# How the background steps of the first attention layer are dealt over the attention loop

## The reference

```python
def gqa_attend(q, k, v):
    s = jnp.einsum('bqhgd,bkhd->bhgqk', q, k).astype(jnp.float32) * (GQA_HEAD_DIM ** -0.5)
    p = jax.nn.softmax(s, axis=-1).astype(v.dtype)
    return jnp.einsum('bhgqk,bkhd->bqhgd', p, v)
...
    k, v, q, g = jnp.split(h @ p["w_in"], cuts, axis=-1)
    q = apply_axial_rope(rms_norm(q.reshape(B, S, GQA_KV_HEADS, GQA_GROUP, GQA_HEAD_DIM), p["q_norm"]), cos, sin)
...
    o = sweep_query_blocks(lambda qb: gqa_attend(qb, k_all, v_all), q).reshape(B, S, GQA_WIDTH)
    y = (o * jax.nn.silu(g)) @ p["w_out"]
```

## Time and profile before

| what | us |
|---|---|
| median of 3 runs | 4112.04 (4110.61 to 4112.57) |
| the profiled execution | 4113.06, of which the span is 4111.2 |
| TensorE busy, whole span | 3764.8 (92%), mean granted clock 0.965 |
| VectorE, ScalarE, GpSimd busy | 1603.5 (39%), 1214.8 (30%), 527.4 (13%) |
| first attention layer's loop, from the first maximum to the last | 1799.6 to 2859.6 |
| one token tile in it (tiles 3 to 8) | 117.9 to 119.4 |
| the last tile, first to last maximum | 94.5 |

### The profile page before, as it was taken

How to read it: one execution, slowest core, us unless ns; L and a number is a source line. 1 busy time by engine, 2 the same in 40 slices (tenths; PEclk the granted TensorE clock), 3 DMA queues, 4 the chain that set the end, 5 groups by cost and what they waited for, 6 DMA issues and landing times.

```text
span 4111.2 us, 56888 instructions
## 1 busy us (share of the span) xinstructions
PE 3764.8 (92%) x24715; PEld 2348.1 (57%) x24715; DVE 1603.5 (39%) x2422; ACT 1214.8 (30%) x2101; POOL 527.4 (13%) x499
## 2 busy tenths in 40 slices
PE   8899999989799999988989888988898999989989
PEld 4566666565477777344555555555554666556654
DVE  2444454543311111733444444444223444444430
ACT  1323323310111111423233333333122444344430
POOL 0211222111000000411001000100112000200001
PEclk9999999999799999998999999998999999999989
DMA  3000000212599999930000000002100000000002
GB/s 106 17 17 22 17 17 12 83 34 103 232 362 367 368 365 350 366 95 16 11 6 16 16 16 16 11 20 97 68 16 11 1 1 12 1 1 1 1 31 72
DMA packets 108049, 346.80 MB, mean 84 GB/s; under 512 B 13351, under 2 KB 39271, under 8 KB 89623
## 3 DMA queue, kind: packets, MB, share of 16 engines
q1 hardware_dynamic: 85862, 284.85, 19.0%
q0 software_dynamic: 9072, 33.03, 2.4%
q10 hardware_dynamic: 12864, 25.27, 1.7%
HBM read 296.94 MB, written 46.19 MB: 83 GB/s over the span
## 4 chain that ended last, share of the span: by engine, by line
PE 77%; DVE 10%; issue 5%; ACT 3%; POOL 3%; DMA 2%; SPq 1%; POOLq 0%; ACTq 0%; DVEq 0%
PE ps L2522 10%; PE ps L2018 8%; PE ps L1613 7%; PE ps L383 7%; PE ps L3226 6%; PE ps L2540 4%; PE ps L2045 4%; PE ps L1630 4%; PE ps L2914 3%; PE ps L1207 3%; DVE sb L1992 2%; PE ps L457 2%; PE ps L3188 2%; POOL sb L1825 2%; PE ps L468 1%
## 5 line engine op out<-in xcount | busy, mean ns | idle before, releaser
L2522 PE MATMUL ps<-sb 128*128 128x512 f32 x960 | 472.5, 610 | 55.4 <-DVE sb L2682 22.1
L2018 PEld LDWEIGHTS ps<-sb 128*128 128x128 f32 x2624 | 299.9, 144 | 340.4 <-ACT sb L2026 130.5
L2026 ACT ACTIVATE sb<-ps 128x512 f32<-128x512 f32 x400 | 238.9, 597 | 797.6 <-PE ps L2018 797.6
L2018 PE MATMUL ps<-sb 128*128 128x128 f32 x2624 | 429.3, 287 | 47.7 <-ACT sb L2002 18.5
L2002 ACT ACTIVATE sb<-ps,sb 128x1280 f32<-128x1280 f32 (+1 forms) x288 | 352.4, 1230 | 143.8 <-DVE sb L1995 140.9
L383 PE MATMUL ps<-sb 128*128 128x512 f32 x704 | 358.9, 625 | 5.1 <-DMA sb<-in_w_in 3.6
L1613 PE MATMUL ps<-sb 128*128 128x256 f32 x1504 | 343.0, 382 | 0.8 <-ACT sb L1645 0.8
L3226 PE MATMUL ps<-sb 96*128 96x512 f32 (+1 forms) x768 | 339.0, 535 | 0.0
L2033 DVE COPY sb<-ps 128x512 f32<-128x512 f32 x256 | 177.1, 692 | 414.0 <-PE ps L2018 413.7
L2045 PEld LDWEIGHTS ps<-sb 128*64 128x64 f32 x5248 | 290.1, 139 | 72.4 <-ACT sb L2026 37.0
L2045 PE MATMUL ps<-sb 128*64 128x128 f32 x5248 | 325.6, 279 | 2.9 <-DVE sb L2033 1.6
(11 more groups left out here) (361 smaller groups left out, 4671.4 us busy)
## 6 DMA issues: line engine op xcount, KB each, us to landing
sb<-in_exp_gate SPq DMA_DIRECT2D x47, 1024.0 KB
sb<-in_exp_up SPq DMA_DIRECT2D x47, 1024.0 KB
sb<-in_exp_down SPq DMA_DIRECT2D x47, 1024.0 KB
sb<-in_l_w_mod ACTq DMA_DIRECT2D x12, 2048.0 KB
d_ys<-sb SPq DMA_DIRECT2D x47, 512.0 KB, 14.4
sb<-d_x SPq DMA_DIRECT2D x32, 512.0 KB, 4.1
sb<-in_w_in SPq DMA_DIRECT2D x22, 512.0 KB, 4.1
sb<-in_x SPq DMA_DIRECT2D x16, 512.0 KB, 5.0
```

Of the source, the lines that this page charges most:

```text
L2018: ins = k.pe.e.transpose(k.bank(6)[:, 128 * j:128 * j + 128], self.Pb[g % 2][:, 1280 * b + 128 * c:1280 * b + 128 * c + 128], k.f(C_ID, 128))
L2026: k.act.e.activation(self.PT[:, xs[0]:xs[-1] + 1, :], k.bank(6)[:, 0:128 * len(xs)].rearrange("p (j t) -> p j t", j=len(xs)), ACT.Copy).th ...
L2522: ins = pe.e.matmul(k.bank(5), lhs[:, kk, :], w[:, kk, 512 * half:512 * half + 512], start=kk == 0, stop=kk == 7)
```

## The change

The step costs `cost` (us of TensorE) are given for the six kinds that use bank 5. `dealt` goes through the same steps in the same order. Each such step is put at the place where its share of the summed cost falls. If the step in front of it is in that place already, it goes to the next one, except that the steps kk > 0 of a product may stay with their neighbours. All other steps stay at the place of the step in front of them: an evacuation directly behind its last matmul, and likewise loads, squares, roots and `silu`. The order of TensorE's background steps stays the same; the slots' gaps no longer count.

```diff
+    cost = dict(mmq=0.9, mmg=0.9, mmo=0.9, turnh=0.55, qturn=0.5, gT=0.5)
+
+    def dealt(todo, count):
+
+
+        steps = [s for slot in todo for s in slot]
+        kinds = [s[1] if s[0] == "lat" else s[0] for s in steps]
+        total = sum(cost.get(x, 0.0) for x in kinds)
+        out, place, last, done = [[] for _ in range(count)], 0, -1, 0.0
+        for step, kind in zip(steps, kinds):
+            if kind in cost:
+                place = max(place, int(done / total * count))
+                if place == last and not (kind[:2] == "mm" and step[3]):
+                    place = min(place + 1, count - 1)
+                last = place
+                done += cost[kind]
+            out[place].append(step)
+        return out
...
-                    yield from (s for slot in todo[place * len(todo) // max(last, 1):] for s in slot)
-                    todo, place, last = window(n), 0, sum(places(x) for x in range(g, g + 8))
+                    todo, place = dealt(window(n), sum(places(x) for x in range(g, g + 8))), 0
...
-                    for slot in todo[place * len(todo) // last:(place + 1) * len(todo) // last]:
-                        yield from slot
+                    if place < len(todo):
+                        yield from todo[place]
                     place += 1
```

More of the change, by code:

```diff
@@ L2486, in everything @@
             yield from slot
-        todo, place, last = [], 0, 0
+        todo, place = [], 0
         for g in range(-1, G + 1):
```

## The result

The changed kernel takes 4052.36 us (median; 4046.87 to 4056.85 over four runs) against 4111.93 before: a ratio of 0.9857, with a 95% interval of 0.9845 to 0.9870. That is 59.6 us less, where 42 were forecast. The profiled execution is the fastest of the four, with a span of 4045.0 us, 66.2 less than the one before.

What follows compares the result with a forecast made beforehand. TensorE, 77% of the chain, bounds the kernel; 17.8 us of a middle tile's 119.3 are waits and clock. 6 x 7.3 + 9 + 3 - 13 = 42.8 us saved gives 4070; range 4048 to 4098, the forecast's own 4054 to 4084.

Steps and rivals of the forecast that it cites:

- rival 2: First-layer loop: no clock fall in any tile and the small load comes early; 66 us saved, 4046; chance 0.10.
- The sum without the clock, 111.0 us: Middle tile after the change: eight pairs' TensorE work and waits plus 0.6 us for single-step places, at full clock.
- Bounds of a tile: Middle tile: 110.4 us up to 114.3 with 6.6 us of low clock costing 3.3; 112 taken, 7.3 saved (5 to 9).
- Rival 1: Every tile: the clock still falls, on dense products; tiles save 5 us, last loses 18; 20 saved, 4092; chance 0.17.
- 3 saved: Tiles 0 and 1 together: three waits of about 0.85 us go; 3 us saved (0 to 5).
- 9 saved: Tile 2, 37 places: pairs come to 108.5 us, 112 with some low clock, against 120.9; 9 saved (5 to 12).
- The last tile: Tile 9: steps without cost collapse together and row tile 2's load waits behind 4 MB; 13 us lost (5 to 20).
- one gap of about 26 us between two maxima: Last tile, sign in the timeline: one such gap, with ScalarE's square released by a DMA about when the 4 MB land.
- if that gap is above 35 us: Last tile: a gap between two maxima above this size was to show that the sum is wrong.
- 2.4 + 58.5: Last tile after the third pair's scores start: 2.4 us for low clock, then five pairs of 11.70 us.
- Rival 4: Last tile: thin steps keep the clock low, 7.7 us in each of six pairs, 46 more; 4116 or 4134; chance 0.05.
- Rival 3: Middle tiles: evacuations already have own slots and waits only move; a tile saves 2 us; 4112; chance 0.08.

Runs made afterwards that it cites:

- the run with the weights behind the load: Changed kernel with SyncE's 4 MB gate-weight load issued right behind row tile 2's load instead of ahead of it: 4047.31 us, ratio 0.9849.
- joined evacuations: Kernel before, slots and spacing kept, each evacuation moved into its last matmul's slot, opening tile's late key steps one slot earlier: 4039.72 us, ratio 0.9819.
- the mixed run: Changed kernel with tiles 0 to 2 dealt, tiles 3 to 9 laid out by slots with each evacuation in its last matmul's slot: 4031.85 us, ratio 0.9803.
- no bank rule: Changed kernel without the rule sending a step that needs the bank of the step in front to the next place: 4090.41 us, ratio 0.9959.

## Why the prediction was right, and where it was off

The forecast was 42 us less, with savings of 28 to 58 counted as its own; 59.6 were measured. The time, 4052, lies inside the whole range of 4048 to 4098 but just outside the forecast's own 4054 to 4084, on the side of rival 2 (no fall in any middle tile, and the small load early: 4046). The first half of rival 2 is what happened in this profile, the second is not. The terms did not cancel: all four were too low, by 5.2, 8.1, 4.8 and 2.9 us (tiles 3 to 8, 0 and 1, 2, and 9), 21 us in the profile's loop. So the waits and the 4 MB load were rightly seen, but what they and the clock are worth only roughly.

**Middle tiles.** The sum without the clock, 111.0 us, measured 110.83, and no pair was off by more than 0.9 us. The step that failed is the clock's: "Bounds of a tile: 110.4 (without the last 0.6) and 111.0 + 3.3 = 114.3; I take 112". The changed kernel's profile has no fall in tiles 3 to 8, and the run with the weights behind the load shows that one, when it comes, lasts 3.4 us and costs 1.7, where I had 6.6 and 3.3. That makes 8.2 saved a tile instead of 7.3. Rival 1 was wrong in size even where its mechanism appears. The Trainium skill (TensorE: Matmul & The Clock Gate, Part 4: PE-mode transpose) says that a transpose does not count as PE-busy in the same way, and by it I had written that the fall would stay in every tile. It did not: in the three profiles with joined evacuations a middle tile has nothing but transposes for five places, some 6.7 us, and kept the full clock in 15 of 18 tiles. What these runs show is that the clock falls at the same thin stretch in some tiles and not in others; what decides it stays open.

**Tiles 0 to 2** were undersized: "3 saved" was 11.1 and "9 saved" was 13.8. I had priced the waits and left the clock out of tiles 0 and 1. It was 0.88 and 0.93 there and is 1.00 and 0.98 after; TensorE's busy time, which grows with a low clock, fell by 5.0 and 2.6 us at the same number of instructions. That the gain of tile 0 needs no dealing is shown by the joined evacuations, with 49.9 us. Of tile 1's 3.4 us some is luck of the clock: the same dealing took 73.5 us there in the mixed run, 0.7 less than before. In tile 2 busy time fell by 5.6 of 13.8.

**The last tile** went as written, with its cause shown by moving one load: 19 us from issue to use behind 4 MB, 104.6 us for 94.5. The forecast spoke of "one gap of about 26 us between two maxima" and called its sum wrong "if that gap is above 35 us". The gap is 36.0, followed by one of 11.8, so by that sign the sum failed. The sign was at odds with the working: a maximum of 2.83 us that ends at 2804 starts 36 us behind the tile's first one, at 2765.06. About 26 is the distance from the second pair's scores to the third's (25.3 measured), while the maximum itself waits on VectorE behind `mean` 2. The two gaps together are 47.8 us, where my times gave 46.9 (2809.5 less the tile's first scores at 2762.6). After them I had 2.4 + 58.5 = 60.9 us, and 56.8 were measured. The low clock cost nothing more, for it was back at full in these five pairs. And only three of them hold three product steps and take 11.7 us; two hold two steps and take 10.84, one step of 0.86 less. Hence 10 lost instead of 13. Rival 4 fell: the later pairs ran at 10.8 to 11.7 us.

**Rival 3** ("the dealing does not do what it says") was nearest to something true. The change promises dealing by TensorE's time; what saved most of the time in the middle tiles is its side effect, that steps without a cost stay where the step in front of them is. I had listed it first among the waits, but did not ask what it would give alone. Moved alone it gives more than the change (0.9819 against 0.9857).

## What to carry to other kernels

When background work is threaded through a loop by a common list, put each evacuation directly behind the matmul that it empties, ahead of the loop's own next copy: the bank's round trip then hides behind one group of transposes. The same placing can be wrong for steps that wait long. A rule that gives them no cost piled a DMA's consumers up in front of the last tile's copies and maxima (10 to 11 us), and a table switch in front of the exponentials (0.8 us a tile); for the GpSimd root, moving it gave nothing. Before filling all of a loop evenly, look for stretches that are bound by another engine's pace: with joined evacuations the three turns cost nothing there.

## What the hardware showed that I had not expected

The granted clock fell in the same stretch of the same kernel in some tiles and not in others: of the tiles 3 to 8, two in four of the profiles with the layouts of 108.8 to 110.8 us, one in one, none in three. In the two layouts that stretch the turns' pair (no bank rule, evacuations in the next place) it fell in five and in all six. In the short layouts one fall lasted 3.4 us and cost 1.6 to 1.7; without the bank rule a longer one cost 2.5. The kernel before took 4110.61 to 4112.57 us in its first runs, but 4104.3 to 4116.6 over all chips, and the changed one spreads by 10 us, so differences under 5 us are read from stretches of the profile and not from medians.
